# Router logits in four column groups, and the routing stage's p tiles turned and split early

## The reference

```python
x = x + mixed @ P['w_out'][i]
x = x + hier_moe(rmsnorm(x, P['g_ffn'][i]), P['router_g'][i], P['router_g_b'][i],
                 P['router_e'][i], P['router_e_b'][i], P['w_gate_up'][i], P['w_down'][i])
x = x + jax.nn.sigmoid(rmsnorm(x, P['g_ple'][i]) @ P['w_ple_gate'][i]) * (p[i] @ P['w_ple_proj'][i])

def hier_moe(h, router_g, router_g_b, router_e, router_e_b, w_gate_up, w_down):
    lg = (h @ router_g + router_g_b)                 # 4 groups
    pg = softmax(lg); p_sel, g_sel = top_k(pg, 1)
    le = (h @ router_e + router_e_b)                 # 16 experts, 4 a group
    ...                                              # two experts of the chosen group, their weights
    return sum over the chosen experts of down(silu(g) * u * gate)
```

## Time and profile before

| | us |
|---|---|
| median of 3 runs | 1946.05 |
| lowest and highest run | 1943.7 and 1951.98 |
| profiled execution | 1933.52 |
| its span, first to last instruction | 1931.7 |
| PE busy | 1772.5 (92%) |
| DVE busy | 880.7 (46%) |
| ACT busy | 601.8 (31%) |
| POOL busy | 414.9 (21%) |
| mean granted clock of TensorE | 0.957 |

### The profile page before, as it was taken

How to read it: one execution, slowest core, us unless ns; L and a number is a source line. 1 busy time by engine, 2 the same in 40 slices (tenths; PEclk the granted TensorE clock), 3 DMA queues, 4 the chain that set the end, 5 groups by cost and what they waited for, 6 DMA issues and landing times. The chain is left out here.

```text
span 1931.7 us, 27172 instructions
## 1 busy us (share of the span) xinstructions
PE 1772.5 (92%) x10466; PEld 1445.8 (75%) x10467; DVE 880.7 (46%) x1021; ACT 601.8 (31%) x997; POOL 414.9 (21%) x281
## 2 busy tenths in 40 slices
PE   6999999889999979988999997998789998997897
PEld 5877888777877847776888885887668777785685
DVE  5201766202144047721788224312536879901774
ACT  4201222131111136631455214112434443442432
POOL 3001111111111010002100012000046565652430
PEclk8999999999999989999899999998889999998998
DMA  5212222222455221033674333222646768733553
GB/s 191 84 33 68 84 73 94 96 73 94 144 178 178 70 86 38 17 131 124 207 202 129 131 126 149 82 71 100 254 134 240 281 246 301 291 115 121 196 175 98
DMA packets 114924, 265.90 MB, mean 138 GB/s; under 512 B 11971, under 2 KB 58643, under 8 KB 114828
## 3 DMA queue, kind: packets, MB, share of 16 engines
q1 hardware_dynamic: 98572, 209.11, 32.3%
q0 software_dynamic: 8320, 30.43, 4.7%
q10 hardware_dynamic: 7936, 25.01, 3.6%
HBM read 192.95 MB, written 71.55 MB: 137 GB/s over the span
## 5 line engine op out<-in xcount | busy, mean ns | idle before, releaser
L2045 DVE TENSOR_TENSOR ex_wlo<-ex_raw,ex_whi 128x1024 fp32r<-128x1024 f32 x96 | 144.1, 1515 | 0.0
L2041 DVE CAST ex_whi<-ex_raw 128x1024 fp32r<-128x1024 f32 x90 | 95.4, 1066 | 85.5 <-DMA ex_raw<-experts 74.4
L275 PE MATMUL rest_p<-hi_h,whi_in 128*128 128x512 f32 (+1 forms) x480 | 122.9, 365 | 12.1 <-POOL wlo_in L894 6.7
L2570 PE MATMUL ex_gu<-ex_whi,ex_xh 128*128 x280 | 114.9, 410 | 14.8 <-issue 8.4
L275 PE MATMUL rest_p<-lo_h,whi_in 128*128 128x512 f32 (+1 forms) x480 | 120.7, 360 | 0.0
L275 PE MATMUL rest_p<-hi_h,wlo_in 128*128 128x512 f32 (+1 forms) x480 | 120.7, 360 | 0.0
L2571 PE MATMUL ex_gu<-ex_wlo,ex_xh 128*128 x280 | 110.7, 395 | 0.0
L2572 PE MATMUL ex_gu<-ex_whi,ex_xl 128*128 x280 | 110.6, 395 | 0.0
L275 PEld LDWEIGHTS rest_p<-hi_h,whi_in 128*128 128x128 f32 x480 | 80.9, 191 | 34.4 <-POOL wlo_in L894 7.6
L865 ACT ACTIVATE rest_out<-rest_p 128x1024 f32<-128x1024 f32 x20 | 20.5, 1026 | 256.2 <-PE rest_p L275 256.2
L894 POOL TENSOR_TENSOR wlo_in<-wraw_in,whi_in 128x1024 fp32r<-128x1024 f32 x18 | 43.7, 2430 | 221.7 <-ACT whi_in L859 221.6
(11 more groups left out here) (380 smaller groups left out, 4107.2 us busy)
## 6 DMA issues: line engine op xcount, KB each, us to landing
ex_raw<-experts SPq DMA_DIRECT2D x96, 512.0 KB, 6.5
wraw_in<-units SPq DMA_DIRECT2D x36, 512.0 KB, 4.1
y_slots<-ex_y ACTq DMA_DIRECT2D x35, 512.0 KB, 4.3
rest<-rest_out SPq DMA_DIRECT2D x20, 640.0 KB, 6.1
scan_e<-erow SPq DMA_DIRECT2D x32, 256.0 KB, 4.5
xtok<-conv_tok SPq DMA_DIRECT2D x10, 640.0 KB, 3.3
z_x<-x SPq DMA_DIRECT2D x10, 512.0 KB, 4.0
ao_gate<-rest SPq DMA_DIRECT2D x8, 640.0 KB, 4.8
```

What stands on the lines that cost most here:

```text
L275: mm = pe.matmul(out[:, n, 0:size], w[:, kk, :], h[:, kk, c:c + size], start=(kk == 0 and w is whi and h is hi), stop=(kk == ktiles - 1 an ...
L2041: eng.tensor_copy(self.hi[:, e % 2, n, :], self.raw[e % 2][:, n, :]).then_inc(self.w_hi[n], 1)
L2045: eng.tensor_tensor(self.lo[:, e % 2, n, :], self.raw[e % 2][:, n, :], self.hi[:, e % 2, n, :].bitcast(F32), ALU.subtract).then_inc(self.w ...
L2570: pe.matmul(gu[s][:, :], xh[s][:, kk, :], hi, start=(kk == 0), stop=False)
```

## The change

In `stage_out_route` the router's weights become the stationary operand: 32 columns (20, and 12 of zeros that POOL writes before the load), with the turned tile's 128 tokens moving. The eight channel tiles go to four column groups, c % 4, each into its own 32 partitions of a PSUM tile `nr_pp` (`parts(t)`). ACT copies that to SBUF (`part_copy(t)`, `nr_part`), and one fp32 matmul with a picking matrix (`nr_pick`, a one at 32q + j for column j) adds the four groups and turns the result to tokens by 20 (`logits(t)`). The order on PE becomes: products of tile t, logits(t-3), parts(t-2), turn(t-1).

In `stage_route` PE turns pair t+2 of p directly behind product t, for t = 0, 1, 2; the token block comes behind product 5 instead of product 3; ACT splits those pairs ahead of the copies and takes the six expert units behind copies 2 to 7; DVE's `p_rest` of pairs 2 to 4 go into the slot chain, and its six expert remainders come last.

```diff
-        rw = k.at("nr_rw", [P, KT, 20], F32, O_ST + 6 * 4096)
-        rb = k.at("nr_rb", [P, 20], F32, O_ST + 6 * 4096 + 640)
-        norm = TileNorm(k, "nr", d["g_ffn"], O_R2 + 10 * 4096, O_ST + 6 * 4096 + 736)
+        rw = k.at("nr_rw", [P, KT, 32], F32, O_ST + 6 * 4096)
+        rb = k.at("nr_rb", [P, 20], F32, O_ST + 6 * 4096 + 1024)
+        pick = k.at("nr_pick", [P, 20], F32, O_ST + 6 * 4096 + 1312)
+        part = k.at("nr_part", [P, 2, P], F32, O_ST + 6 * 4096 + 1408)
+        norm = TileNorm(k, "nr", d["g_ffn"], O_R2 + 10 * 4096, O_ST + 6 * 4096 + 1120)
...
+        pp = ctx.enter_context(nc.psum_tensor("nr_pp", [P, P], F32))
...
-            sp.dma_start(rw[:, :, :], d["router"]).then_inc(par_in, 16)
+            sp.wait_ge(rw_zero, 1)
+            sp.dma_start(rw[:, :, 0:20], d["router"]).then_inc(par_in, 16)
...
+            pool.memset(rw[:, :, :], 0.0).then_inc(rw_zero, 1)
...
+            def part_copy(t):
+                act.wait_ge(parted, t + 1)
+                if t >= 2:
+
+                    act.wait_ge(routed, t - 1)
+                act.activation(part[:, t % 2, :], pp[:, :], ACT.Copy).then_inc(part_copied, 1)
+
             for t in range(NT):
...
                     norm.square(act, t, by_ktile(x1[:, t, :]), of_tile(turned_h2, t))
+                if t >= 2:
+                    part_copy(t - 2)
                 if t:
                     act.wait_ge(turned, t)
                     act.activation(of_tile(turned_h2, t - 1), tp[:, :, :], ACT.Copy).then_inc(copied, 1)
+            part_copy(NT - 1)
...
+            def parts(t):
+
+                pe.wait_ge(copied, t + 1)
+                if t:
+
+                    pe.wait_ge(part_copied, t)
+                for c in range(KT):
+                    q = c % 4
+                    mm = pe.matmul(pp[32 * q:32 * q + 32, :], rw[:, c, :], turned_h2[:, c, t * P:(t + 1) * P], start=(c < 4),
+                                   stop=(c >= 4))
+                mm.then_inc(parted, 1)
+
             def logits(t):
-                pe.wait_ge(copied, t + 1)
-                for c in range(KT):
-                    mm = pe.matmul(lp[:, t, :], turned_h2[:, c, t * P:(t + 1) * P], rw[:, c, :], start=(c == 0),
-                                   stop=(c == KT - 1))
-                mm.then_inc(routed, 1)
+                pe.wait_ge(part_copied, t + 1)
+                pe.matmul(lp[:, t, :], part[:, t % 2, :], pick[:, :], start=True, stop=True).then_inc(routed, 1)
 
...
                     pe.wait_ge(par_in, 48)
+                    pe.wait_ge(picked, 3)
+                if t >= 3:
+                    logits(t - 3)
                 if t >= 2:
-                    logits(t - 2)
+                    parts(t - 2)
                 if t >= 1:
                     turn(t - 1)
+            logits(NT - 3)
+            parts(NT - 2)
+            turn(NT - 1)
             logits(NT - 2)
-            turn(NT - 1)
+            parts(NT - 1)
             logits(NT - 1)
 
         @block.vector
+            for q in range(1, 4):
+                a = ident[:, 0:20] if q == 1 else pick[:, :]
+                dve.tensor_tensor(pick[:, :], a, ident[:, 32 * q:32 * q + 20], ALU.add).then_inc(picked, 1)
+                dve.wait_ge(picked, q)
...
                                           scalar=float(P), in1=off[:, :, :], op0=ALU.mult, op1=ALU.add))
+            p_rest(2)
             for n, a in enumerate((a1, a2)):
                 step(dve.tensor_tensor(w16[:, :, :], a[:, :, :], off[:, :, :], ALU.mult))
                 step(dve.tensor_reduce(slot[:, n, :], w16[:, :, :], AX.X, ALU.add))
+            p_rest(3)
...
+            p_rest(4)
...
             dve.wait_ge(found, 1)
             dve.tensor_copy(r.token[:, :], pp[0][:, 160:160 + NBLK]).then_inc(token_set, 1)
-            for m in range(2, NT // 2):
-                p_rest(m)
-                ew.split_lo(dve, 0, 2 * m - 4)
-                ew.split_lo(dve, 0, 2 * m - 3)
+            for n in range(6):
+                ew.split_lo(dve, 0, n)
...
             p_split(1)
-            for t in range(4):
-                ew.split_hi(act, 0, t)
+            for t in range(NT):
+                if t < 3:
+                    p_split(t + 2)
                 copy(t)
-            ew.split_hi(act, 0, 4)
-            ew.split_hi(act, 0, 5)
-            for m in range(2, NT // 2):
-                p_split(m)
-                if m >= 3:
-                    copy(2 * m - 2)
-                    copy(2 * m - 1)
-            copy(NT - 2)
-            copy(NT - 1)
+                if 2 <= t < 8:
+                    ew.split_hi(act, 0, t - 2)
...
-            for t in range(4):
+            for t in range(6):
                 product(t)
+                if t < 3:
+                    turn(t + 2)
             for n in range(2):
                 pe.wait_ge(hot_ready, n + 1)
                 for t in range(NT):
                     mm = pe.matmul(pp[0][:, 160:160 + NBLK + 1], row_hot[n][:, t, :], token_at[n][:, t, :],
                                    start=(n == 0 and t == 0), stop=(n == 1 and t == NT - 1))
             mm.then_inc(found, 1)
-            for m in range(2, NT // 2):
-                turn(m)
-                if m >= 3:
-                    product(2 * m - 2)
-                    product(2 * m - 1)
-            product(NT - 2)
-            product(NT - 1)
+            for t in range(6, NT):
+                product(t)
 
         @block.gpsimd
         def _(pool):
```

More of the change, by code:

```diff
@@ L2077, in stage_out_route @@
             "nr_routed")
+        rw_zero, picked, parted, part_copied = k.sems(ctx, "nr_rw_zero", "nr_picked", "nr_parted", "nr_part_copied")
         ident = k.const[:, C_ID:C_ID + P]
```

## The result

The changed kernel took 1927.69 us, the median of 4 runs (1926.49 to 1935.61), against 1949.01 for the kernel before beside it: ratio 0.9912, 95% interval 0.9883 to 0.9941. Timed once more later it took 1933.99 (9 runs), ratio 0.9935 (0.991 to 0.996). On the median that the forecast starts from, 1946.05, the two ratios are 1929 and 1933. It is faster by more than half a per cent in the first comparison, and most likely in the second, by the amount forecast, 12.9 us, or a few more.

A forecast was written before the change was run, and what follows sets the result against it. Wholly busy PE was taken to bound the output projection, and hand-overs to PE plus a 5.56 us stall the routing. 5.5 + 2.8 + 4.6 = 12.9 us off the median 1946.05 gives 1933, range 1926 to 1943.

The forecast's parts named there:

- Middle tiles: Output projection, before the last tile of products is done: shorter logits work on PE saves 5.5 us.
- The block: One tile's parts on PE, eight matmuls in four column groups beside each other: 0.73 us.
- the price of entering and leaving: Extra PE time around a tile's parts in four column groups: 0.29 us together.
- ACT's copy: ACT's added copy of the parts to SBUF, once per tile: 0.27 us, hidden behind other work.
- End of the stage: Output projection's last turn and logits: the turn no longer waits behind logits, at the lower clock; 2.8 us less.
- Routing: Routing stage: early turns and splits of p shorten the 5.56 us wait ahead of product 4 to 2.3; 4.6 less.
- my bound: Routing stage's upper limit: 6.9 us saved if the first store doesn't hold product 4 at all.
- rival C: Routing stage gives 1.5 to 2.7 us, not 4.6, through the late store or the clock; 1936 us, chance 0.22.
- The sum: Whole kernel: 5.5 + 2.8 + 4.6 = 12.9 us saved, giving 1933 us; chance 0.60.
- The base: Saving set against the runs' median of 1946.05 us; the profiled execution of 1933.52 was 12.5 under it.
- B: Output projection: column groups don't run beside each other, a tile's parts take 2.07 us; 0.8 left, 1945 us, chance 0.09.
- D: Middle tiles of the output projection: PE's clock falls behind thinner matmuls; slower, 1961 us with 16 a tile, chance 0.04.

The follow-up runs named there:

- routing only: The kernel before with the changed routing stage; 1948.36 us, ratio 0.9992.
- one group: The changed kernel with all eight channel tiles sent to a single column group; 1944.06 us, ratio 0.9976.
- turn first: The kernel before with the last tile's turn moved ahead of the logits of the tile before it; 1953.99 us in a single run.
- two buffers more: The changed kernel with products 2 and 3 copied into buffers of their own, the first gather waiting for their stores; 1935.99 us, ratio 0.9917.
- logits only: The changed kernel with the whole routing stage as it was before; 1941.68 us, ratio 0.996.
- units first: The changed kernel with own buffers for products 2 and 3 and the two weight units loaded ahead of p; 1932.13 us, ratio 0.9908.
- units first with short warm: The changed kernel with own buffers for products 2 and 3, weight units loaded before p, and warm-ups before counting and product 0; 1935.43 us, ratio 0.9931.
- late buffers with short warm: The changed kernel with own buffers for products 2 and 3, copies 8 and 9 where p lay, two warm-ups before product 0; 1935.81 us, ratio 0.9937.

## Why the prediction was right, point by point

**Middle tiles.** Forecast 5.5 less; measured 10.8 for the stage without the 4.5 of its end, 6.3. This part doesn't vary: from the first turn to the last residual addition it is 106.7 or 106.8 us in the three traces with the old logits and 100.5 in the ten with the new ones. The mechanism was right. The block took 0.58 instead of 0.73: seven times 0.15 is 1.05 us, about the difference. The term that was too large is the price of entering and leaving, 0.29 from the earlier trace rows; measured it is 0.58 - 4 x 0.111 = 0.14. Part of what I read as that price in the earlier trace rows was the first products behind, which run slowly after the turn too. The adding product (0.22 for 0.21) and ACT's copy (0.26 to 0.28 for 0.27) were right, and ACT's order hid the copy as said. The Trainium skill, "TensorEngine Tiling (Array Packing)", Key Properties, says that a change of tiling mode drains TensorE; the trace leaves 0.14 us or less for entering and leaving, and doesn't show what it is spent on.

**End of the stage.** Forecast 2.8 less; measured 12.8 to 8.3 (last residual addition at 1329.90), 4.5. The step that failed is the turn that "ends at 1336.6 at today's 1.95" and the block at twice its passes: I carried the lower clock over from the earlier trace rows. In the changed kernel's trace it stayed at 1.00 through the end. That is not sure to happen. The end has the same code in ten traces (all but before, routing only, one group, turn first). In four the last turn and parts take 1.09 and 0.64, and in six 1.20 to 1.41 and 1.08, the clock falling within the turn; these end 0.8 to 1.0 us later. The old end varies as well, 11.7 and 12.8 us in two traces of the same code. So the gain at the end lies between 2.5 us (11.7 to 9.2) and 4.5, and the forecast of 2.8 is inside that; the 4.5 sets a short trace of the new end against a long one of the old.

**Routing.** Forecast 4.6 less; measured 4.3, and 4.5 the second time. What is late next is the store, as said; with it out of the way 1.9 to 2.0 more are gained (two buffers more), close to the 2.3 of my bound (6.9 - 4.6), though 0.9 of that is the clock in one of the two comparisons. One thing went otherwise: the forecast had product 0 at its old place in the stage, 10.95 in, and a wait of 2.3 ahead of product 4. It started at 11.8, because the weights landed later, twelve of its matmuls ran at the lower clock instead of nine, and the wait was 0.38. Both end at the same store, so the sum held: by luck of a gate that doesn't move, not by the steps ahead of it. The routing-only run is the case that the forecast described, product 0 at 11.1 and a wait of 2.69; there rival C's clock came with the wait, and 1.7 was gained, not 4.6.

**The sum.** 15.1 us by the traces, 12.9 forecast, 12.6 and 17.1 by the two ratios. The 15.1 is at the upper end of what the traces allow: against the routing-only trace, logits only gains 8.9 us in its stage (118.5 to 109.6), and routing only gains 1.7 in its own, 10.6 in all. That the sum came out this close is in part luck: the middle was sized 0.8 too low, and of the end's 4.5 and the routing's 4.3 neither came by the steps that were forecast. The two halves alone are worth 0.4% and 0.1% by their runs, 0.5% together, with intervals of 0.3% each; 15.1 us is 0.8%. Nothing shows them to work on each other beyond that.

**The base.** Setting the sum against the median, and not against the profiled 1933.52, was what kept the forecast right. Why that execution was 12.5 us fast can be read in part. It had no slow operation on POOL (some 10 us, below), and its output projection began earlier: the first product stands at 1193.4, and in the changed kernel's trace at 1196.7, up to 1203.4 in the others, ahead of which no code differs. The timed runs have no trace, so this is argued, not shown.

**Rivals.** B is refuted by the block of 0.58 and by one group. D is refuted by the clock of 1.00 in the middle. C's mechanism is real (routing only), but didn't come in the changed kernel's two traces.

## What to carry to other kernels

Where a matmul with few moving columns stands in the path of a full TensorE, exchange the operands, so that the wide side moves, and spread the contraction over column groups; a short product at the end adds the groups. The exchange alone gained nothing here; the groups did. Put whatever needs another engine's copy one tile later. Where a store gates a buffer, find out first when it lands, since work moved up in front of it only becomes a wait; and set a forecast against the median, not against the one execution that was profiled.

## What was not expected of the hardware

**A POOL operation of ten microseconds.** The product `ex_hid` (128x256, usually 0.7 to 1.8 us) took 10.1 to 11.3 us once in nine of the fourteen traces and 6.7 once in one more (turn first), each time the 20th of the 35. Four have none over 1.80: before, units first, units first with short warm, late buffers with short warm. In those four the experts' first and last turn are 337.8 to 338.1 us apart, in the ten others 346.7 to 351.0. Turn first has 347.8 with only 6.7 for the operation, so the operation's length isn't the whole of the delay. The second trace of the changed kernel:

```profile
1605.03 10.46 POOL L2550 TENSOR_TENSOR ex_hid<-ex_up,ex_silu 128x256 f32<-128x256 f32 x1 [7.98 <-ACT ex_up L2667]
```

It is about as large as the whole change and as the scatter of the runs of one kernel (10 to 20 us), though whether it makes that scatter isn't shown: the timed runs have no trace. Only the changed kernel has two traces, and both have it; whether it goes with the execution or with the program isn't shown either. It stands in kernels with and without the change, so the change isn't what brings it. Its cause stays open.

**The clock at low and at high load.** At the end of the output projection's stage, the window of the kernel before:

```profile
1332.00:1343.00 11.00, 8.60 (x46) 7.85 (x43) 1.57 (x3) 2.50 (x4) 0.55 (x1) 0.62 0.15 48
```

PE was busy 8.60 of 11 us with its clock at 0.62 on average; after, 3.70 of 7 us at 1.00. The turn-first run has 4.00 us at 1.00 with 1.91 busy, and then, through the 20-column passes, 6 us wholly busy at 0.51:

```profile
1343.00:1347.00 4.00, 1.91 (x18) 1.67 (x18) 1.44 (x2) 2.10 (x3) 0.55 (x1) 1.00 0.00 0
1347.50:1353.50 6.00, 6.00 (x30) 6.00 (x29) 0.00 (x0) 0.92 (x1) 0.00 (x0) 0.51 0.26 85
```

So the busy share of these stretches doesn't tell their level: 107.00 of 107.00 us busy at 1.00 in the middle, 6.00 of 6.00 at 0.51 here. The same code kept the clock in four traces and lost it in six; with one group, where PE is busier, the last turn still took 1.09. What decides it stays open.
